# The last phase of a two-block layer: the sums of squares of keys and queries as two products of high and low parts, in the five passes 0 to 4, with the low parts made by GpSimd

## The chip, the cores and the metric

The kernel runs on one core of one Trainium2 chip. The metric is the device time of one execution, in microseconds (us). Lower is better. The program names five engines: TensorE (PE in the profile, PEld for its weight loads), VectorE (DVE), ScalarE (ACT), GpSimd (POOL) and SyncE (SP), which issues loads and stores. Each engine works through its own list of instructions strictly in order; semaphores are the only ties between lists. An instruction that waits therefore holds up everything behind it on its engine.

## The reference, cut to what matters

Two transformer blocks follow each other. The change lies in the second one, where queries and keys of every head are normalised over their 64 features before attention:

```
NORM_EPS = 1e-6
def rms_norm(t, g):
    tf = t.astype(jnp.float32)
    y = tf * lax.rsqrt(jnp.mean(tf * tf, axis=-1, keepdims=True) + NORM_EPS)
    return (y * g.astype(jnp.float32)).astype(t.dtype)
...
u = h @ w_in[i]
dq, dk, dv, bq, bk, bv, z = jnp.split(u, IN_SPLIT_IDX, axis=-1)
dq = rms_norm(dq.reshape(B, S, DIFF_HEADS, 2, HEAD_DIM), diff_q_norm_g[i])
dk = rms_norm(dk.reshape(B, S, DIFF_HEADS, 2, HEAD_DIM), diff_k_norm_g[i])
...
bq = rms_norm(bq.reshape(B, S, DIL_HEADS, HEAD_DIM), dil_q_norm_g[i])
bk = rms_norm(bk.reshape(B, S, DIL_HEADS, HEAD_DIM), dil_k_norm_g[i])
```

The sequence has 1024 positions, four differential heads (two queries and two keys of 64 features each) and eight dilated heads.

## The kernel before

**The phase.** The function `mixers_phase` runs eight passes p = 0 to 7, each over two times 64 features: passes 0 to 3 are the differential heads (DIFF = 4), passes 4 to 7 pairs of dilated heads. A pass has 16 units x = 0 to 15. A unit of pass p does the attention of pass p and, woven in, the projections of the next pass q = p + 1. The opening, p = -1, is 16 units that hold only the projections and key work of q = 0. The order of every engine's list is written out by hand: each engine has a loop over p and x, and small tables say what a unit holds.

**The projections.** For every q there are eight groups of 8 steps: GK0, GK1 (keys, two halves of 512 positions), GQ0, GQ1 (queries), GV0, GV1 (values), GZ0, GZ1 (gates). A step is `gemm_k`, three matmuls of 128x512 in type fp32r (lines 79 to 81: high by high, high by low, low by high). `share(q, x)` says which steps stand in a unit. For q of 1 and more GK0 ends in unit 1, GK1 with the first step of unit 3, GQ0 in unit 4, GQ1 in unit 6. In the opening the order is GK0, GQ0, GV0, GZ0, GK1, GQ1, GZ1, GV1; the first group has already been made by the phase before.

**The weights.** They come through two buffers. `W.split` on POOL turns one loaded tile of 128x1024 into a high part (line 135) and a low part (line 137); PE waits for it at a tile's first step, and the split waits until the tile that used the buffer before is done. In the opening, `opening = {1: 0, 2: 1, 3: 2, 4: 3, 5: 4, 7: 5, 9: 6}` sets in which unit POOL splits which; split 0 delivers the tile of the third group, GV0. In later passes a split stands in units 0, 4, 8 and 12.

**Keys and queries.** When a group of them is complete, ACT empties its PSUM bank (`empty`): the square into the tile `sq` (line 2472), a plain copy into `un` (line 2474, which frees the bank and counts `gfree`). PE sums the squares over 64 features by one matmul with the 0/1 matrix K.pairs (item "S", line 2262, plain fp32). ACT scales the sum (`halve`, line 2523) and forms the inverse root by Ln, Exp and a square (`inverse_root`, lines 2530 to 2541). DVE takes one correction step and scales `un` (`scale`, lines 2718 to 2722). POOL splits `un` in a high part (line 2195) and a low part (line 2201), in `split_rows`, and PE multiplies keys and queries (`keys`, line 2312; `scores`, lines 2347 and 2350). `sums_of` places the four S items of q in units 3, 4, 5 and 7 (in the opening 4, 5, 6 and 8), at the unit's head. `normed_at` places `scale` and `split_rows` one unit later each. `is_late` lists the items that stand behind the unit's second projection step instead.

**What else counts.** A unit's attention on DVE is `add` (line 2704), the maxima of `keys` for the next pass (line 2741) and `weigh` (line 2778); on PE it ends with `values` (line 2366), which needs the `weigh` of the unit before. `un`, `sq` have two buffers each, used in turn by the running number c of the group among keys and queries (`number_of`).

Of the kernel before, what the change touches and what calls it, by code (L numbers as in the profile page):

```python
# [5 lines left out]
F32 = mybir.dt.float32  # L6
F32R = mybir.dt.float32r
BF16 = mybir.dt.bfloat16
ALU = mybir.AluOpType
ACT = mybir.ActivationFunctionType  # L10
P = 128
D = 1024
T = 1024
META = 16
L = META + T
KT = D // P
# [1886 lines left out]

def mixers_phase(nc, K, u_hi, u_lo, strips, pt, S, V_p, acc0, o1, x1, row_of):

# [16 lines left out]
    order = lambda q: [GK0, GQ0, GV0, GZ0, GK1, GQ1, GZ1, GV1] if q == 0 else list(range(8))  # L1922
    place = lambda q, g: order(q).index(g)
    number_of = lambda q, g: 4 * q + [n for n in order(q) if n <= GQ1].index(g)
    tile_of = lambda q, g: place(q, g) if q == 0 else 4 * q + 4 + g // 2
# [47 lines left out]
    roots = {it: n for n, it in enumerate(it for it in number if it[0] in "SN")}  # L1973
    is_late = lambda p, x, it: it[0] == "E" and x == 6 or it[0] in ("D", "P", "EB", "EP") or it[0] == "T" and (p < 0 or x == 13)

# [27 lines left out]
    with ExitStack() as ctx:  # L2003
# [22 lines left out]
        stored = [s(f"stored{i}") for i in range(4)]  # L2026
        tok_ok = s("tokens")
        rootx, invx, scalex, addx_ok, sqx_ok, sumx = (s(n) for n in ["rootx", "invx", "scalex", "addx", "sqx", "sumx"])
# [152 lines left out]
        def _(pool):  # L2181
            def split_rows(q, g):
# [18 lines left out]
                nc.gpsimd.tensor_tensor(lo, new, hi.bitcast(F32), ALU.subtract).then_inc(lo_ok, 1)  # L2201

            def key_tokens(q, i):

                pool.wait_ge(lo_ok, 4 * q + 4)
                pool.wait_ge(mx_full, base(q) + 6)
                source = (k_hi, k_lo)[i][:, q % 2].bitcast(F32)
                nc.gpsimd.tensor_copy(turned(tok[:, i]), classes(source)).then_inc(tok_ok, 1)

            opening = {1: 0, 2: 1, 3: 2, 4: 3, 5: 4, 7: 5, 9: 6}  # L2210
            for p in range(-1, PASSES):
                q = p + 1
                for x in range(U):
                    if q < PASSES and x in normed_at(q):
                        split_rows(q, normed_at(q)[x])
                    if q < PASSES and not diff(q) and x in (13, 14):
                        key_tokens(q, x - 13)
                    if p < 0:
                        if x in opening:
                            W.split(pool, 0, 0, opening[x])  # L2220
                    elif x == 0:
                        W.split(pool, 0, 0, 4 * p + 7)
                    elif x in (4, 8, 12) and q < PASSES:
                        W.split(pool, 0, 0, 4 * q + 3 + x // 4)
# [9 lines left out]
        def _(pe):  # L2234
# [15 lines left out]
            def extra(it):  # L2250
# [9 lines left out]
                if kind == "S":  # L2260
                    pe.wait_ge(sq_ok, number_of(q, g) + 1)
                    last = nc.tensor.matmul(bank, K.pairs[:, :], sq[:, number_of(q, g) % 2], start=True, stop=True)
                if kind == "N":
# [147 lines left out]
            for p in range(-1, PASSES):  # L2411
                q = p + 1
# [49 lines left out]
        def _(act):  # L2462
            def empty(q, g):
# [5 lines left out]
                if g <= GQ1:  # L2469
                    c = number_of(q, g)  # L2470
                    least(act, un_ok, c - 1)
                    nc.scalar.activation(sq[:, c % 2], gbank(n), ACT.Square).then_inc(sq_ok, 1)
                    least(act, lo_ok, c - 1)
# [207 lines left out]
        def _(dve):  # L2681
# [178 lines left out]
            nc.vector.memset(mn[:, :], 0.0).then_inc(cleared, 1)  # L2860
            dve.wait_ge(cleared, 1)
            for j in range(2):
                last = nc.vector.memset(ek[64 * j:64 * j + 2, :].bitcast(F32), 1.0)
# [283 lines left out]
def program(nc, d, s):  # L3147
    K = Kernel(d, s)
    with ExitStack() as top:
# [36 lines left out]
        with ExitStack() as two:  # L3186
# [7 lines left out]
            with ExitStack() as c2:  # L3194
# [9 lines left out]
                W.base = W.base + 2 * KT  # L3204
                mixers_phase(nc, K, h_hi, h_lo, strips, pt, S, V_p, acc0, o1, x1, mix_row)
                clear_semaphores(nc)
# [104 lines left out]
```

## Time and profile before

| | before |
|---|---|
| median of 3 runs | 2913.04 us (2912.51 to 2915.86) |
| the profiled execution: time, span | 2912.82 us, 2911.0 us |
| mean granted clock of TensorE | 0.98 of 2.4 GHz |
| PE busy over the span | 2761.9 us (95%) |
| DVE, ACT, POOL busy | 1708.0 us (59%), 1045.7 us (36%), 935.9 us (32%) |
| the phase `mixers_phase` | about 1890 to 2720 us of the span |

A timeline row gives the start in us from the span's start, the duration in us, the engine, the line, the operation, the tiles (out<-in) with shape and count, and in brackets how long the engine stood idle before it and for whom. Matmuls are pipelined: the record of one overlaps the next, so what a matmul costs is the distance from start to start, not its duration. A plain fp32 matmul leaves two records. Busy shares are means over a stretch; what a change is worth is read from the waits.

### The profile page before, as it was taken

Reading aid. Unit: us, or ns where it says so; the run is one execution under the profiler, and the core shown is the slowest. Engines: PE = TensorE matmul, PEld = TensorE weight load, DVE = VectorE, ACT = ScalarE, POOL = GpSimd, SP = SyncE. Lnnn points to the kernel's source line nnn. Section 1 sums busy time; section 2 is a strip of 40 time slices with the busy share of each in tenths; the row PEclk is TensorE's granted clock in tenths of the full one; section 3 lists DMA queues with packets and bytes.
Section 4 is the critical chain, followed back from the end, with each engine's and each line's share of the span. In section 5 each row is a group of like instructions: output and inputs, shape, how many; then the busy total and the mean of one; then the engine's idle time right before and its main releaser. Section 6 shows DMA issues by size and latency. Waiting matters only on the chain. (4 is left out here: it accounts for less than half of the span.)

```text
span 2911.0 us, 39453 instructions
## 1 busy us (share of the span) xinstructions
PE 2761.9 (95%) x15534; PEld 2115.5 (73%) x15534; DVE 1708.0 (59%) x2674; ACT 1045.7 (36%) x1735; POOL 935.9 (32%) x549
## 2 busy tenths in 40 slices
PE   6999999999999899999999999979999999998899
PEld 5879797977777677777766887755666666665677
DVE  5787878786022344444454115666776667775586
ACT  4342524343010233333333002346666644344232
POOL 1233323332664122211212334542122234341465
PEclk8999999999999899999999999989999999999999
DMA  4131413244432111111113225421110111103544
GB/s 166 60 84 66 94 66 83 71 80 155 165 118 91 37 52 52 50 47 48 34 44 135 82 80 183 137 86 36 40 43 27 43 43 44 43 30 113 173 150 112
DMA packets 113751, 237.32 MB, mean 82 GB/s; under 512 B 9120, under 2 KB 52896, under 8 KB 113568
## 3 DMA queue, kind: packets, MB, share of 16 engines
q1 hardware_dynamic: 63312, 172.93, 17.9%
q10 hardware_dynamic: 50256, 61.87, 7.3%
q8 instruction: 124, 2.03, 0.3%
q14 instruction: 59, 0.48, 0.1%
HBM read 190.66 MB, written 44.11 MB: 81 GB/s over the span
## 5 line engine op out<-in xcount | busy, mean ns | idle before, releaser
L79 PE MATMUL psum<-u_h,w_hi 128*128 128x512 f32 (+2 forms) x2624 | 1012.7, 386 | 25.0 <-PEq L46 7.3
L80 PE MATMUL psum<-u_h,w_hi 128*128 128x512 f32 (+2 forms) x2624 | 968.4, 369 | 0.0
L81 PE MATMUL psum<-u_h,w_lo 128*128 128x512 f32 (+2 forms) x2624 | 966.3, 368 | 0.0
L135 POOL TENSOR_SCALAR w_hi<-w_raw 128x1024 fp32r<-128x1024 f32 x212 | 241.6, 1140 | 1468.6 <-ACTq L1324 519.1
L79 PEld LDWEIGHTS psum<-u_h,w_hi 128*128 128x128 f32 x2624 | 497.8, 190 | 156.1 <-issue 69.3
L137 POOL TENSOR_TENSOR w_lo<-w_raw,w_hi 128x1024 fp32r<-128x1024 f32 x212 | 546.1, 2576 | 17.7
L81 PEld LDWEIGHTS psum<-u_h,w_lo 128*128 128x128 f32 x2624 | 497.8, 190 | 71.8
L80 PEld LDWEIGHTS psum<-u_h,w_hi 128*128 128x128 f32 x2624 | 498.5, 190 | 69.3 <-issue 9.0
L2545 ACT ACTIVATE a_exp<-a_exp 128x1024 f32<-128x1024 f32 x96 | 101.6, 1058 | 161.9 <-DVE a_exp L2708 88.3
L1349 ACT ACTIVATE f_exp<-psum 128x1024 f32<-128x1024 f32 (+4 forms) x112 | 82.2, 734 | 192.9 <-PE psum L1207 94.0
L1445 DVE CUSTOM_DVE_ANT_0 f_junk<-psum,f_decay,f_max 128x512 f32<-128x512 f32 (+2 forms) x96 | 60.3, 666 | 134.4 <-PE psum L1230 121.1
L2704 DVE TENSOR_TENSOR a_exp<-psum,a_strips 128x1024 f32<-128x1024 f32 x64 | 78.2, 1222 | 74.2 <-PE psum L2350 73.5
L603 ACT ACTIVATE decay<-decay,ssd_small 128x128 f32<-128x128 f32 x256 | 78.4, 389 | 102.2 <-DVE decay L803 97.8
L79 PE MATMUL psum<-yo_hi,w_hi 128*128 128x512 f32 x256 | 100.8, 394 | 6.0 <-DVE yo_lo L1003 3.4
L80 PE MATMUL psum<-yo_lo,w_hi 128*128 128x512 f32 x256 | 100.4, 392 | 0.0
L81 PE MATMUL psum<-yo_hi,w_lo 128*128 128x512 f32 x256 | 100.2, 391 | 0.0
L1253 PE MATMUL psum<-f_exp,f_v 128*64 128x512 f32 (+4 forms) x448 | 89.0, 474 | 3.0 <-ACT f_exp L1349 3.0
L2195 POOL CAST a_khi<-a_un 128x512 fp32r<-128x512 f32 x16 | 15.6, 974 | 229.7 <-DVE a_un L2722 229.7
L2551 ACT ACTIVATE a_biased<-a_biased,a_negmax 128x1024 f32<-128x1024 f32 x60 | 68.5, 1144 | 45.0 <-DVE a_negmax L2748 45.0
L1003 DVE TENSOR_TENSOR yo_lo<-yo_raw,yo_hi 128x512 fp32r<-128x512 f32 x32 | 31.2, 1045 | 90.5 <-ACT yo_hi L951 90.5
L1460 DVE TENSOR_TENSOR f_sum<-f_sum,f_exp 128x800 f32<-128x800 f32 (+2 forms) x96 | 77.6, 809 | 7.1 <-ACT f_exp L1349 6.0
L1445 DVE CUSTOM_DVE_ANT_0 f_junk<-psum,f_decay 128x512 f32<-128x512 f32 (+4 forms) x128 | 48.8, 433 | 55.8 <-PE psum L1230 37.8
(433 smaller groups left out, 4419.3 us busy)
## 6 DMA issues: line engine op xcount, KB each, us to landing
w_raw<-in_w_all SPq DMA_DIRECT2D x212, 512.0 KB, 3.5
sums_rows<-s_acs ACTq DMA_DIRECT2D x32, 512.0 KB, 8.8
f_decay<-s_nc SPq DMA_DIRECT2D x16, 520.0 KB, 5.4
s_y<-conv_out ACTq DMA_DIRECT2D x16, 512.0 KB, 2.9
yo_raw<-s_y ACTq DMA_DIRECT2D x8, 1024.0 KB, 10.3
a_strips<-in_strips SPq DMA_DIRECT2D x8, 960.0 KB, 5.4
x_tok<-in_x SPq DMA_DIRECT2D x8, 512.0 KB, 8.2
s_xT<-xT SPq DMA_DIRECT2D x8, 512.0 KB, 6.0
```

The costliest lines, as they stand in the source:

```text
L79: nc.tensor.matmul(out, w_hi[:, k], a_hi, start=(k == 0 and first), stop=False)
L80: nc.tensor.matmul(out, w_hi[:, k], a_lo, start=False, stop=False)
L81: return nc.tensor.matmul(out, w_lo[:, k], a_hi, start=False, stop=(k == kk - 1 and final))
L135: self.nc.gpsimd.tensor_scalar(self.hi[:, r], self.raw[:, r], 1.0, 1.0, ALU.mult, ALU.mult).then_inc(self.hi_done, 1)
L137: self.nc.gpsimd.tensor_tensor(self.lo[:, r], self.raw[:, r], self.hi[:, r].bitcast(F32), ALU.subtract).then_inc(self.ready, 1)
L603: last = nc.scalar.activation(seg[:, d % 3, r], seg[:, d % 3, r], ACT.Exp, scale=-1.0, bias=sm[:, g, 0, d, r:r + 1])
L1253: last = nc.tensor.matmul(ps[64 * j:64 * j + 64, OB + q0:OB + 512], V[0:n, kb, j], pt[0:n, x % 2, j, q0:512], start=(kb == 0), stop=(kb == ...
L1349: nc.scalar.activation(pt[0:n, x % 2, :, q0:512], src[:, :, q0:512], ACT.Exp, scale=0.125).then_inc(exp_ok, 1)
L1445: last = nc.vector.tensor_tensor_reduce(out=junk[:, j, o:o + e - a], in0=ps[:, MX + 512 * j + o:MX + 512 * j + o + e - a], in1=ncb[:, j, a ...
L1460: nc.vector.tensor_tensor(to, to, src, ALU.add).then_inc(acc_ok, 1)
L2545: nc.scalar.activation(pt[:, X % 3], pt[:, X % 3], ACT.Exp, scale=0.125).then_inc(exp_ok, 1)
L2704: tt(pt[:, X % 3], bank, strips[:, p % 2:p % 2 + 1, o:o + 512].to_broadcast([P, 2, 512]), ALU.add).then_inc(add_ok, 1)
```

## The change

For every q up to DIFF (0 to 4, so for twenty of the thirty-two groups; `halved(q)`), the sum of squares is taken in two matmuls of type fp32r instead of one in fp32. ACT writes the square into the tile `tok`, which is fp32r and holds a rounded, high part. POOL forms the square again in full from the copy `un` (into `sq`) and subtracts the high part, which gives the low part (`squares_low`). PE multiplies both with `exact`, an fp32r copy of K.pairs that DVE makes once, in a free piece of the tile u_h. These S items become late: they stand behind the second projection step of their unit. PE waits for `low_ok`, POOL waits for `gfree`.

```
-    is_late = lambda p, x, it: it[0] == "E" and x == 6 or it[0] in ("D", "P", "EB", "EP") or ...
+    is_late = lambda p, x, it: it[0] == "S" and halved(it[1]) or it[0] == "E" and x == 6 or it[0] in ("D", "P", "EB", "EP") or ...
...
+            def squares_low(q, g):
+                c = number_of(q, g)
+                pool.wait_ge(sq_ok, c + 1)
+                pool.wait_ge(gfree, 8 * q + place(q, g) + 1)
+                nc.gpsimd.tensor_tensor(sq[:, c % 2], un[:, c % 2], un[:, c % 2], ALU.mult).then_inc(low_ok, 1)
+                pool.wait_ge(low_ok, 2 * c + 1)
+                nc.gpsimd.tensor_tensor(tok[:, 1, 512 * (c % 2):512 * (c % 2) + 512], sq[:, c % 2],
+                                        tok[:, 0, 512 * (c % 2):512 * (c % 2) + 512].bitcast(F32), ALU.subtract).then_inc(low_ok, 1)
...
                     if q < PASSES and x in normed_at(q):
                         split_rows(q, normed_at(q)[x])
+                    for g, k in share(q, x) if q < PASSES and halved(q) else []:
+                        if k == KT - 1 and g <= GQ1 and (q, g) != (0, GK1):
+                            squares_low(q, g)
+                    if (q, x) == (0, 5):
+                        squares_low(0, GK1)
...
                 if kind == "S":
-                    pe.wait_ge(sq_ok, number_of(q, g) + 1)
-                    last = nc.tensor.matmul(bank, K.pairs[:, :], sq[:, number_of(q, g) % 2], start=True, stop=True)
+                    c = number_of(q, g)
+                    if halved(q):
+                        pe.wait_ge(const_ok, 1)
+                        pe.wait_ge(low_ok, 2 * c + 2)
+                        for i in range(2):
+                            last = nc.tensor.matmul(bank, exact, tok[:, i, 512 * (c % 2):512 * (c % 2) + 512], start=(i == 0), stop=(i == 1))
+                    else:
+                        pe.wait_ge(sq_ok, c + 1)
+                        last = nc.tensor.matmul(bank, K.pairs[:, :], sq[:, c % 2], start=True, stop=True)
...
-                    nc.scalar.activation(sq[:, c % 2], gbank(n), ACT.Square).then_inc(sq_ok, 1)
+                    squares = tok[:, 0, 512 * (c % 2):512 * (c % 2) + 512] if halved(q) else sq[:, c % 2]
+                    nc.scalar.activation(squares, gbank(n), ACT.Square).then_inc(sq_ok, 1)
...
+            nc.vector.tensor_copy(exact, K.pairs[:, :])
```

The first place is POOL's list at the phase's start. Before, it begins with the weight splits:

```order
L2180 UNCONDITIONAL_BRANCH
L135 TENSOR_SCALAR w_hi<-w_raw 128x1024
L137 TENSOR_TENSOR w_lo<-w_raw,w_hi 128x1024
L135 TENSOR_SCALAR w_hi<-w_raw 128x1024
L137 TENSOR_TENSOR w_lo<-w_raw,w_hi 128x1024
```

In the changed kernel the two pairs of `squares_low` for GK0 and GQ0 (lines 2209 and 2211) stand there first:

```order
L2181 UNCONDITIONAL_BRANCH
L2209 TENSOR_TENSOR a_sq<-a_un 128x512
L2211 TENSOR_TENSOR a_tokens<-a_sq,a_tokens 128x512
L2209 TENSOR_TENSOR a_sq<-a_un 128x512
L2211 TENSOR_TENSOR a_tokens<-a_sq,a_tokens 128x512
L135 TENSOR_SCALAR w_hi<-w_raw 128x1024
L137 TENSOR_TENSOR w_lo<-w_raw,w_hi 128x1024
```

So split 0, the weights of GV0, has moved behind the squares of GQ0.

The second place is POOL's list in pass 0, from the split of the keys GK0 in unit 4 to the split of the queries GQ1 in unit 8. Before:

```order
L2195 CAST a_khi<-a_un 128x512
L2201 TENSOR_TENSOR a_klo<-a_un,a_khi 128x512
L135 TENSOR_SCALAR w_hi<-w_raw 128x1024
L137 TENSOR_TENSOR w_lo<-w_raw,w_hi 128x1024
L2195 CAST a_khi<-a_un 128x512
L2201 TENSOR_TENSOR a_klo<-a_un,a_khi 128x512
L2195 CAST a_qhi<-a_un 128x512
L2201 TENSOR_TENSOR a_qlo<-a_un,a_qhi 128x512
L2195 CAST a_qhi<-a_un 128x512
L2201 TENSOR_TENSOR a_qlo<-a_un,a_qhi 128x512
```

And now (lines 2196 and 2202 are the old 2195 and 2201):

```order
L2196 CAST a_khi<-a_un 128x512
L2202 TENSOR_TENSOR a_klo<-a_un,a_khi 128x512
L2209 TENSOR_TENSOR a_sq<-a_un 128x512
L2211 TENSOR_TENSOR a_tokens<-a_sq,a_tokens 128x512
L135 TENSOR_SCALAR w_hi<-w_raw 128x1024
L137 TENSOR_TENSOR w_lo<-w_raw,w_hi 128x1024
L2196 CAST a_khi<-a_un 128x512
L2202 TENSOR_TENSOR a_klo<-a_un,a_khi 128x512
L2196 CAST a_qhi<-a_un 128x512
L2202 TENSOR_TENSOR a_qlo<-a_un,a_qhi 128x512
L2209 TENSOR_TENSOR a_sq<-a_un 128x512
L2211 TENSOR_TENSOR a_tokens<-a_sq,a_tokens 128x512
```

The pair for GQ0 stands between the split of GK0 and the weights, and the pair for GQ1 behind the split of GQ0.

The third place is PE's list in the same pass, unit 3. Before, the S matmul stands ahead of scores and key products:

```order
L2366 MATMUL psum<-a_exp,a_v 128x512
L2262 MATMUL psum<-a_sq,pairs 128x512
L2347 MATMUL psum<-a_qhi,a_khi 128x512 x2
L2347 MATMUL psum<-a_qlo,a_khi 128x512 x2
L2347 MATMUL psum<-a_qhi,a_klo 128x512 x2
L2350 MATMUL psum<-a_queryrows,a_keyrows 128x512 x2
```

Now two matmuls stand behind the second projection step:

```order
L2335 MATMUL psum<-a_khi,a_qlo 128x512 x2
L79 MATMUL psum<-u_h,w_hi 128x512
L80 MATMUL psum<-u_h,w_hi 128x512
L81 MATMUL psum<-u_h,w_lo 128x512
L79 MATMUL psum<-u_h,w_hi 128x512
L80 MATMUL psum<-u_h,w_hi 128x512
L81 MATMUL psum<-u_h,w_lo 128x512
L2282 MATMUL psum<-a_tokens,u_h 128x512 x2
```

All S items of passes 0 to 4 move in this way, four in each; in unit 8 of the opening the item also falls behind the first key products.

## Rows read from the trace of the kernel before

**Rows 1.** Busy time in two stretches: opening of the last phase, and one pass.

```profile
core 0: us, PE busy (x) PEld busy (x) DVE busy (x) ACT busy (x) POOL busy (x), PEclk, DMA share, GB/s
1890.00:1990.00 100.00, 77.47 (x300) 50.21 (x299) 67.81 (x114) 46.79 (x77) 36.13 (x24) 0.90 0.25 88
1990.00:2090.00 100.00, 99.14 (x481) 64.94 (x480) 68.72 (x133) 63.08 (x97) 22.84 (x16) 1.00 0.10 33
```

**Rows 2.** Timeline of PE in unit 4 of pass 0, and one pass later.

```profile
2012.32 1.02 PE L2262 MATMUL psum<-a_sq,pairs 128*128 128x512 f32 x2
2013.27 0.50 PE L2347 MATMUL psum<-a_qhi,a_khi 64*128 64x512 f32 x2
...
2015.10 0.50 PE L79 MATMUL psum<-u_h,w_hi 128*128 128x512 f32 x1
2015.43 0.39 PE L80 MATMUL psum<-u_h,w_hi 128*128 128x512 f32 x1
2015.66 0.39 PE L81 MATMUL psum<-u_h,w_lo 128*128 128x512 f32 x1
...
2112.07 1.02 PE L2262 MATMUL psum<-a_sq,pairs 128*128 128x512 f32 x2
```

**Rows 3.** Timeline at the phase's start: weight split, second drain, next projection.

```profile
1892.45 2.38 POOL L137 TENSOR_TENSOR w_lo<-w_raw,w_hi 128x1024 fp32r<-128x1024 f32 x1
...
1906.44 0.59 ACT L2474 ACTIVATE a_un<-psum 128x512 f32<-128x512 f32 x1
...
1906.97 0.80 PE L79 MATMUL psum<-u_h,w_hi 128*128 128x512 f32 x1
```

**Rows 4.** Instructions of lines 2195 and 2201 on POOL: min/median/max in ns.

```profile
L2195 POOL CAST a_khi<-a_un x16: 611/1086/1497, 1941.3 to 2589.6; 128x512 fp32r<-128x512 f32 x16
...
L2201 POOL TENSOR_TENSOR a_klo<-a_un,a_khi x16: 1262/1406/2067, 1942.0 to 2590.8; 128x512 fp32r<-128x512 f32 x16
```

**Rows 5.** Timeline of pass 0 around the drains, splits and sums of squares.

```profile
2011.89 0.59 ACT L2474 ACTIVATE a_un<-psum 128x512 f32<-128x512 f32 x1
...
2018.56 1.27 POOL L2201 TENSOR_TENSOR a_klo<-a_un,a_khi 128x512 fp32r<-128x512 f32 x1
...
2019.31 1.10 PE L2262 MATMUL psum<-a_sq,pairs 128*128 128x512 f32 x2 [0.33 <-ACT a_sq L2472]
2019.87 0.60 ACT L2474 ACTIVATE a_un<-psum 128x512 f32<-128x512 f32 x1 [0.70 <-POOL a_klo L2201]
...
2032.49 1.29 POOL L2201 TENSOR_TENSOR a_qlo<-a_un,a_qhi 128x512 fp32r<-128x512 f32 x1
```

**Rows 6.** Timeline of the opening's second half.

```profile
1943.26 0.60 ACT L2474 ACTIVATE a_un<-psum 128x512 f32<-128x512 f32 x1 [1.42 <-POOL a_klo L2201]
...
1951.86 1.02 PE L2262 MATMUL psum<-a_sq,pairs 128*128 128x512 f32 x2
...
1954.51 0.50 PE L2312 MATMUL psum<-a_khi,a_qhi 64*128 64x512 f32 x2 [1.63 <-POOL a_klo L2201]
...
1959.86 0.75 DVE L2741 CUSTOM_DVE_ANT_0 a_biased<-psum,a_strips,a_max 128x512 f32<-128x512 f32 x1
...
1977.93 0.63 PE L2279 MATMUL psum<-ident,a_maxrows 128*128 128x128 f32 x4 [3.51 <-DVE a_maxrows L2797]
```

**Rows 7.** Timeline of PE behind an idle stretch in the opening.

```profile
1944.49 1.25 PE L2262 MATMUL psum<-a_sq,pairs 128*128 128x512 f32 x2 [2.64 <-ACT a_vT L2523]
...
1946.38 0.63 PE L81 MATMUL psum<-u_h,w_lo 128*128 128x512 f32 x1
...
1948.87 0.39 PE L81 MATMUL psum<-u_h,w_lo 128*128 128x512 f32 x1
```

**Rows 8.** Timeline of DVE and POOL where both work on SBUF tiles.

```profile
2019.77 1.61 DVE L2778 SCALAR_TENSOR_TENSOR a_exp<-a_exp,neglam 128x512 f32<-128x512 f32 x1
...
2020.93 2.72 POOL L137 TENSOR_TENSOR w_lo<-w_raw,w_hi 128x1024 fp32r<-128x1024 f32 x1
...
2031.20 0.75 DVE L2778 SCALAR_TENSOR_TENSOR a_exp<-a_exp,neglam 128x512 f32<-128x512 f32 x1
```

More of the change, by code:

```diff
@@ L1901, in _, with mixers_phase @@
             split(KT - 1)
-def mixers_phase(nc, K, u_hi, u_lo, strips, pt, S, V_p, acc0, o1, x1, row_of):
+def mixers_phase(nc, K, u_hi, u_lo, exact, strips, pt, S, V_p, acc0, o1, x1, row_of):
     PASSES, DIFF, U, SPAN = 8, 4, 16, 2 * T - P
@@ L1923, in mixers_phase @@
     place = lambda q, g: order(q).index(g)
+    halved = lambda q: q <= DIFF
     number_of = lambda q, g: 4 * q + [n for n in order(q) if n <= GQ1].index(g)
@@ L1973, in mixers_phase @@
     roots = {it: n for n, it in enumerate(it for it in number if it[0] in "SN")}
-    is_late = lambda p, x, it: it[0] == "E" and x == 6 or it[0] in ("D", "P", "EB", "EP") or it[0] == "T" and (p < 0 or x == 13)
+    is_late = lambda p, x, it: it[0] == "S" and halved(it[1]) or it[0] == "E" and x == 6 or it[0] in ("D", "P", "EB", "EP") or it[0] == "T" and (p < 0 or x == 13)
     def scored(p, x):
@@ L2026, in mixers_phase @@
         stored = [s(f"stored{i}") for i in range(4)]
-        tok_ok = s("tokens")
+        tok_ok, low_ok = s("tokens"), s("squares_low")
         rootx, invx, scalex, addx_ok, sqx_ok, sumx = (s(n) for n in ["rootx", "invx", "scalex", "addx", "sqx", "sumx"])
@@ L3204, in program @@
                 W.base = W.base + 2 * KT
-                mixers_phase(nc, K, h_hi, h_lo, strips, pt, S, V_p, acc0, o1, x1, mix_row)
+                mixers_phase(nc, K, h_hi, h_lo, uh[:, 2 * KT * T:2 * KT * T + P], strips, pt, S, V_p, acc0, o1, x1, mix_row)
                 clear_semaphores(nc)
```

## The prediction

> **What bounds the kernel now.** I read first the busy shares by stretch, then the timeline of every engine in two places: the opening of the phase, and one whole pass, with the waits beside each row. In the 100 us from 1990 on, which is one pass, PE is busy for 99.14 us at a granted clock of 1.00, DVE for 68.72, ACT for 63.08 and POOL for only 22.84 [rows 1]. So in the passes PE is the bound: each microsecond taken from its list comes back, and each one in which it must stand still is lost. The opening is another matter. There PE is busy for 77.47 of 100 us, and the end is set by a chain that goes PE, ACT, DVE, POOL and back [rows 1]. The passes repeat: the S of unit 4 stands at 2012.32 and, one pass later, at 2112.07 [rows 2], so what I work out for pass 0 holds for the four passes p = 0 to 3 which make q = 1 to 4; the opening makes q = 0.
>
> **What is taken from PE.** The S matmul starts at 2012.32 and the next one at 2013.27, so it takes 0.95 us of PE's list [rows 2]. An fp32r matmul of the same 128x512 takes 0.23, the distance from 2015.43 to 2015.66 [rows 2]; two are 0.46. The saving is 0.49 for each item, 1.96 for each of the four passes. One old wait of 0.33 for ACT's square goes too [rows 5]. That makes -2.3 for a pass, if the low parts are there in time.
>
> **What POOL's two instructions cost.** The trace has no product of a tile with itself on POOL. The nearest row is the subtraction of 128x512 on the same engine, 1262 ns at best and 1406 in the median; the one-input cast of the same shape has 611 at best, and that is my lower bound for either instruction, the 2067 of the slowest subtraction the upper one [rows 4]. A product of two inputs is nearest to the subtraction, and I take 1.3 for each, 2.6 for the pair: between 1.3 and 4.1.
>
> **The opening, first wait.** POOL's list is in order, and split 0, the weights of GV0, now stands behind the pair for GQ0. That pair waits for ACT's copy of GQ0, which ends at 1906.44 + 0.59 = 1907.03; before, POOL had the weights done at 1892.45 + 2.38 = 1894.83, and PE began GV0 at 1906.97 [rows 3]. Now: 1907.1 + 2.6 for the pair + 1.1 and 2.4 for the split (its second half took 2.38 [rows 3]; its first half lies between the end of a split at 2018.56 + 1.27 [rows 5] and the second half's start at 2020.93 [rows 8]) + 0.2 between them gives 1913.4. PE waits 6.4 us there. The group holds the sums that the second half of the normalised input depends on, which DVE and ACT then work through while PE waits for them, so nothing takes this back: +6.4. If each instruction of the pair were as cheap as the cast it would be 5.0, with slow ones 7.9.
>
> **The opening, second wait.** From here on I use the times of before, without the 6.4. The pair for GK1 can start when its copy is done, at 1943.26 + 0.60 = 1943.86 [rows 6], and ends at 1946.5. Behind it come in POOL's order the weights (3.5, to 1950.0), the split of GQ0 (0.61 + 1.27, to 1952.0), ACT's copy of GQ1, which waits for that (to 1952.7), its pair (to 1955.3), and the split of GK1 (to 1957.3). Before, the first key products followed that split at 1954.51 [rows 6]. They come 2.8 later. The S of GQ1 stood at 1951.86, before them [rows 6]; now it stands behind them and two steps, at about 1957.3 + 1.0 + 2.4 = 1960.7, with the steps at the slower clock as they are now. From its S to DVE's second maximum, which stands behind the scaling of GQ1, took 1951.86 to 1959.86 [rows 6]; with 0.4 less for the matmul and 1.3 less for waits on the way the maximum comes at about 1967, 7 late. DVE and PE work together until the queries' rows are turned at 1977.93, where PE waits 3.51 us for DVE [rows 6]. On the way DVE has, by its timeline, some 3 us of waits that it can make up (an estimate). That leaves +3.8; I add 0.8 for the shared tiles (below) and take +4.6, between 1 (the casts' price) and 6. The opening costs 6.4 + 4.6 = 11.0. S savings count nothing here, since PE stands idle around them.
>
> **A pass.** Take pass 0.
> - GK1: ACT's copy ended at 2011.89 + 0.59 = 2012.48 [rows 5], now 0.2 later, as ACT serves the later S of GK0 first. The pair ends at 2012.8 + 2.6 = 2015.4. PE begins unit 4 at 2011.84 (2012.32 less 0.49 saved in unit 3), needs 1.83 for scores and keys (2013.27 to 2015.10 [rows 2]) and 1.38 for two steps, six times 0.23, and is at the S at 2015.05: a wait of 0.4.
> - GQ0: its copy waits for the split of GK0, which ends at 2018.56 + 1.27, and is done at 2019.87 + 0.60 = 2020.47 [rows 5]. The pair ends at 2023.1. PE begins unit 5 at 2018.4 (2018.98 as it was, 0.33 before the S at 2019.31 [rows 5], less 0.98 saved, plus the 0.4 of above, rounded) and is at its S 1.13 + 1.38 later, about 2020.8: a wait of 2.3.
> - GQ1: POOL first splits GQ0, which ended at 2032.49 + 1.29 = 2033.8 [rows 5] and is now 0.6 later, as unit 6 is. The pair ends at 2034.4 + 2.7 = 2037.1. PE is at its S at 2031.4 + 1.13 + 1.38 = 2033.9: a wait of 3.1.
> - GK0 has more than a unit of cover and costs nothing.
>
> Together 5.8 of waits against 2.3 of savings: +3.5. With the casts' price for the pair each of the two large waits is 1.3 shorter and the small one gone, and the pass is at +0.5; at 4.1 for the pair it is at +8.
>
> **Two things that waits bring with them.** First the clock. After PE had been idle for 2.64 us, up to 1944.49, its matmuls took 0.63 each, until one at 1948.87 has 0.39 again [rows 7]: the granted clock had gone from 2.4 to 1.2 GHz for some 3.5 us. In these a matmul starts every 0.43 instead of every 0.23, which loses 1.6. The wait of GQ1 is as long as that one; the wait of GQ0 is shorter, and I count it as harmless. I take 1.3 a pass, between 0 and 3.2. Second, tiles that POOL and DVE both work on. DVE's `weigh` took 1.61 us at 2019.77, against 0.75 at 2031.20; it ended only after POOL's first half of a weight split was over, and the second half, begun at 2020.93, took 2.72 instead of the 2.38 above [rows 8, 3]. They hold each other up. In the changed kernel this weight split begins at 2023.1 and ends at about 2026.7, just where DVE has the small rows of unit 5 and scales GK1. The scaling comes up to 2 us later, then unit 6's add, the scaling of GQ0, its split, the pair and the S. Part of it has slack, and I take +1.0, between 0 and 2.
> The Trainium skill, page "SBUF — State Buffer", section "Who interferes with whom", says that a DVE instruction with two SBUF inputs and a GpSimd instruction that reads SBUF fully block each other, whichever issued first. The trace agrees, with the 1.61 us. By that rule alone nothing is shared and the whole 2 us would come through, 4 us more in all than I count.
>
> A pass: 3.5 + 1.3 + 1.0 = 5.8, four of them 23.2. Pass 3, which makes q = 4, has one more cast on POOL between the splits of GQ0 (0.6), so its pair is later by that: +0.6. The copy `exact` on DVE is 128x128 in a stretch where DVE next waits for a load: nothing; without that cover it would be about 0.2.
>
> **The sum.** 11.0 + 23.2 + 0.6 = +34.8 against the profiled execution, 2912.82, gives 2947.6. Its time lies within 0.3 us of the median of the three runs. I say 2947 us, 1.2% slower.
>
> **The rivals.**
> - *The waits of the passes are small; only the opening is slower.* If POOL's pair takes 1.3 to 1.7, a pass is at about +0.5 to +1 and the opening at 5.0 + 1.5: 2912.8 + 6.5 + 3 = 2922. For it speaks the cast's 0.61 [rows 4]; against it that both instructions have two inputs and none such of this shape was under 1.26. Chance 0.11.
> - *The loss is larger, because POOL and DVE block each other everywhere.* The pair itself collides with `scale`, `add`'s successors and `weigh`; by the page's rule every such meeting costs the length of the other's instruction. With 3.4 for the pair, 2 for the shifted weight split and a slow clock behind both waits, a pass costs 3.5 + 2.4 + 2 + 1.6 = 9.5: 2912.8 + 13 + 38 = 2964. DVE has 31 us of free time in a pass [rows 1], which speaks against all of it coming through. Chance 0.15.
> - *Faster.* PE's list gets 20 times 0.49 = 9.8 us shorter, with old waits some 11, and everything else is covered: 2902. It decides at the price of POOL's pair: at 0.5 us a pass would gain 1.1 (the wait of GQ1 would still be 1.0, as PE is at its S 0.5 before POOL starts the pair) and the opening lose 4.3, which is even; only below that is the kernel faster. The cast alone has 0.61 [rows 4]. Chance 0.03.
> - *No change within the measure*: gains of the passes even with the opening's loss, which needs a pass at -2.3 and an opening of 9. Chance 0.03.
>
> **How the numbers follow.** The forecast case, waits of both kinds with 2930 to 2960, has 0.68. A measurement of this kernel can tell about 0.2%, 6 us, from no change. Slower by more: 0.68 + 0.11 + 0.15 = 0.94; within: 0.03; faster: 0.03. The range takes the lower bound of a pass with a quick pair (a pass at 3, the opening at 8: 2933) and goes down to 2929, and up to 2962, which holds about half of the case of blocking; outside remain the first rival and the rest of the second, with the two small ones some 0.2 in all.
>
> **What the profile after would show.** Step by step: PE idle for about 6 us before its first step of GV0, released by POOL's line 137; the pair at 1.3 us each; in each of the passes 0 to 3 waits of PE for POOL's line 2211 in units 4, 5 and 7, near 0.4, 2.3 and 3.1, so some 23 us over the four; matmuls of 0.63 behind the third; DVE's scaling lengthened where the weight split meets it. Wrong would be: a pair much shorter than 2.6; a PE that reaches its S later than I reckon, because DVE holds it up in the scores, which would turn one wait into another; or an opening whose chain has slack that I have not seen.

## The result, and the profile after

The changed kernel takes 2958.43 us (median of 4 runs, 2957.19 to 2959.70) against 2912.78 for the kernel before on the same chip: 1.0155 times as long, 95% interval 1.0139 to 1.0171. The prediction was 2947 us, in a range of 2929 to 2962. The profiled execution took 2957.19 us, with a span of 2955.4 and a mean granted clock of 0.973.

The busy shares of the changed kernel, in the opening and in one pass, answer to [rows 1]:

```profile
core 0: us, PE busy (x) PEld busy (x) DVE busy (x) ACT busy (x) POOL busy (x), PEclk, DMA share, GB/s
1890.00:2001.00 111.00, 77.57 (x271) 51.16 (x272) 60.48 (x103) 40.62 (x68) 43.54 (x31) 0.80 0.22 74
2001.00:2107.00 106.00, 98.08 (x473) 64.49 (x470) 73.13 (x136) 63.86 (x98) 30.62 (x23) 0.97 0.09 28
```

PE does no more work than before; it stands idle for some 8 us of a pass, where it had stood idle for less than one. POOL is busy for only 30.62 of the 106 us, so its load is not what holds PE up, but when its pieces come. The list of PE's waits over the whole phase names the places (line waited at, releaser, us in total, times, longest):

```profile
PE psum L2282 <- POOL a_tokens L2211: 26.4, 9, 5.5
PE psum L2335 <- POOL a_klo L2202: 7.1, 1, 7.1
...
PE psum L79 <- POOL w_lo L137: 6.0, 1, 6.0
...
PE psum L2370 <- ACT a_queryrows L2543: 4.5, 4, 1.1
```

Line 2282 is the new S item. The last row stands at a place that the forecast does not name: the scores (line 2370) wait for ACT four times, once a pass.

**The opening.** The timeline at the phase's start, POOL and PE, answers to [rows 3]:

```profile
1906.58 1.48 POOL L2209 TENSOR_TENSOR a_sq<-a_un 128x512 f32<-128x512 f32 x1 [11.42 <-ACT a_un L2498]
1908.14 1.26 POOL L2211 TENSOR_TENSOR a_tokens<-a_sq,a_tokens 128x512 fp32r<-128x512 f32 x1
...
1910.49 2.34 POOL L137 TENSOR_TENSOR w_lo<-w_raw,w_hi 128x1024 fp32r<-128x1024 f32 x1
...
1912.97 0.76 PE L79 MATMUL psum<-u_h,w_hi 128*128 128x512 f32 x1 [6.04 <-POOL w_lo L137]
1913.54 0.63 PE L80 MATMUL psum<-u_h,w_hi 128*128 128x512 f32 x1
```

PE waits 6.04 us for the weights, where the prediction had 6.4, and the matmuls behind it start 0.43 us apart until 1917.81: the granted clock has gone to the 1.2 GHz level. And in its second half, to be laid beside [rows 6]:

```profile
1954.57 0.70 PE L2282 MATMUL psum<-a_tokens,u_h 128*128 128x512 f32 x2 [3.77 <-POOL a_tokens L2211]
1955.53 2.69 POOL L137 TENSOR_TENSOR w_lo<-w_raw,w_hi 128x1024 fp32r<-128x1024 f32 x1
1955.90 2.87 DVE L2743 SCALAR_TENSOR_TENSOR a_un<-a_un,a_par,a_sq 128x512 f32<-128x512 f32 x1
1967.41 0.79 PE L2335 MATMUL psum<-a_khi,a_qhi 64*128 64x512 f32 x2 [7.10 <-POOL a_klo L2202]
...
1994.14 1.09 PE L2302 MATMUL psum<-ident,a_maxrows 128*128 128x128 f32 x4 [3.51 <-DVE a_maxrows L2821]
```

DVE's scaling of GQ0 takes 2.87 us instead of 0.74 (in the kernel before it starts at 1947.16), because it meets the second half of the weight split, which runs from 1955.53 to 1958.22 and which the pair has pushed into it. The rows are turned at 1994.14, which was 1977.93 before.

**A pass.** Units 4 to 7 of pass 0, all four engines, beside [rows 2, 5, 8]:

```profile
2033.03 0.70 PE L2282 MATMUL psum<-a_tokens,u_h 128*128 128x512 f32 x2
2040.25 0.70 PE L2282 MATMUL psum<-a_tokens,u_h 128*128 128x512 f32 x2 [1.58 <-POOL a_tokens L2211]
2041.20 2.38 POOL L137 TENSOR_TENSOR w_lo<-w_raw,w_hi 128x1024 fp32r<-128x1024 f32 x1
2041.37 2.24 DVE L2814 TENSOR_TENSOR a_lse<-a_logsum,a_negmax 128x8 f32<-128x8 f32 x1
2043.64 0.17 DVE L2816 CAST a_lse_hi<-a_lse 128x8 fp32r<-128x8 f32 x1
...
2049.72 0.50 PE L2370 MATMUL psum<-a_qhi,a_khi 64*128 64x512 f32 x2 [1.12 <-ACT a_queryrows L2543]
...
2052.00 1.27 POOL L2202 TENSOR_TENSOR a_qlo<-a_un,a_qhi 128x512 fp32r<-128x512 f32 x1
2053.23 1.04 POOL L2209 TENSOR_TENSOR a_sq<-a_un 128x512 f32<-128x512 f32 x1
2054.35 1.26 POOL L2211 TENSOR_TENSOR a_tokens<-a_sq,a_tokens 128x512 fp32r<-128x512 f32 x1
...
2055.76 1.19 PE L2282 MATMUL psum<-a_tokens,u_h 128*128 128x512 f32 x2 [3.25 <-POOL a_tokens L2211]
2056.75 0.63 PE L79 MATMUL psum<-u_h,w_hi 128*128 128x512 f32 x1
```

The first row is GK1, with no wait that the view marks (0.26 us in the next pass); GQ0 waits 1.58, GQ1 3.25, with the slow clock behind it. Between them, DVE's sum over eight elements takes 2.24 us: it begins at 2041.37 and ends at 2043.61, POOL's second half of the split at 2043.58. The next one of that size takes 0.17, with POOL idle by then. All that DVE has behind it, the scaling of GK1, the add of unit 6 and with it the exponentials on ACT, is late by these 2 us; ACT copies the query rows behind the exponentials, and for this copy the scores wait.

**A ledger.** To see where each kernel's time differs I take the start of each value product (before: line 2366; one a unit) and subtract its start in the kernel before, counted from the same product. The opening is counted from PE's first matmul of the phase (1890.80 before) to the second value product (1997.54 before); a pass from there on over 16 products, the last over 13. The table gives the opening's length and what each pass is longer, in us, worked out from the PE timelines of the profiled executions. "Keys", "place" and so on are the experiments below.

| kernel | opening | pass 0 | pass 1 | pass 2 | pass 3 |
|---|---|---|---|---|---|
| before | 106.74 | 0 | 0 | 0 | 0 |
| changed | 124.34 | +7.05 | +5.96 | +5.94 | +9.57 |
| opening only | 121.00 | 0.00 | 0.00 | +0.03 | +0.19 |
| passes only | 105.39 | +5.96 | +5.97 | +5.95 | +9.52 |
| keys only | 104.85 | +0.25 | +0.19 | +0.19 | 0.00 |
| place only | 106.88 | +0.79 | +0.70 | +0.69 | +1.48 |
| GK0 alone, at the head | 104.94 | -0.37 | -0.36 | -0.41 | -1.54 |
| split 0 first | 116.48 | +7.15 | +5.95 | +5.94 | +9.63 |
| GQ1 first | 124.56 | +2.52 | +2.53 | +2.53 | +2.95 |
| squares by ACT | 118.91 | +3.69 | +2.09 | +3.62 | +4.33 |
| three of four | 107.29 | +0.34 | +0.34 | +0.34 | +0.27 |
| three, weights in unit 3 | 107.42 | -1.24 | -1.25 | -1.27 | -2.34 |

The unchanged openings lie between 104.85 and 107.42, so a difference under 3 us there says nothing. Counted from the start of the span instead, the second value product stands at 1997.48 to 2000.06 with an unchanged opening, at 2014.99 to 2017.09 with the changed one, and at 2012.97 with split 0 first: a late start of the phase and a short opening go together in part, so a change of the opening is known only to 2 or 3 us by either count. In pass 3 differences of 1.2 us come and go with a wait that has nothing to do with the change. In passes 0 to 2 the table repeats within 0.1 us or so wherever the clock does. For the changed kernel it adds up to 17.6 + 28.5 = 46.1 us; 1.4 of that comes back in passes 4 to 7 (as in experiments 3, 4 and 12, so it is not a gain of the change), and the spans differ by 44.4.

### The profile page after: what moved, and what is told of

Its sections match the earlier page's. It is cut to its first block and busy times, and to the rows that moved or that the text cites. A ratio compares the mean times of both kernels' runs of the same rounds, so it can differ in the third digit from the quotient of the medians.

```text
span 2955.4 us, 39513 instructions
## 1 busy us (share of the span) xinstructions
PE 2769.1 (94%) x15534; PEld 2122.7 (72%) x15534; DVE 1717.1 (58%) x2675; ACT 1047.6 (35%) x1735; POOL 982.7 (33%) x589
## 5 line engine op out<-in xcount | busy, mean ns | idle before, releaser
L388 POOL TENSOR_TENSOR x_dt_decay<-x_dt,ssd_small 128x512 f32<-128x512 f32 (+1 forms) x32 | 36.8, 1152 | 129.3 <-DVE x_dt L789 128.8
```

## The experiments

The lines below are of each kernel's own file, so the same instruction has a number a few apart.

**1. The opening alone.**

```
-    halved = lambda q: q <= DIFF
+    halved = lambda q, g: q == 0
```

> The two products and the low parts only for q = 0, the opening; passes 0 to 3 as before. My theory: the losses of the opening and of the passes are separate and add up. In the trace of the changed kernel the queries' rows of the opening are turned at 1994.14 instead of 1977.93, 16.2 us later, so this kernel should take 2912.8 + 16.2 = 2929.0. Rival 1: the opening costs the 11.0 of my prediction and the rest arises only with the passes: 2924. Rival 2: the passes, with their waits gone, take part of the delay back: 2920 to 2925.

Measured: 2929.75 us, ratio 1.0060 (1.0046 to 1.0073), 18 us above the kernel before on that chip (2911.66). Its passes are at zero in the ledger. So the opening costs 18 us and not the 11.0 of the prediction. The ledger shows 14 to 16 of them in this execution, which entered the phase late (PE's first matmul at 1894.60; over all kernels here it lies between 1890.65 and 1896.49, with no relation to the change that I can see).

**2. The passes alone.**

```
+    halved = lambda q, g: 0 < q <= DIFF
```

> The two products only for q = 1 to 4, made in passes 0 to 3; the opening as before. My theory: what is left of the 45.6 us, 29.4, so 2942. Rival: the passes cost the 23.8 of my prediction: 2936.6. In the trace the waits of the S items for POOL's line 2211 should be as they are now: about 1.6 in unit 5, 3.3 in unit 7, and 1.1 of the scores for ACT's copy of the rows.

Measured: 2938.92 us, ratio 1.0095 (1.0080 to 1.0111): +27.3. The two parts add up, 18.1 + 27.3 = 45.4. The prediction had 23.8 for the passes. Passes 0 to 2 take 5.96 each, 0.2 more than the forecast of 5.8; the rest is pass 3 with 9.5.

**3. Only the keys of q = 1 to 4,** GK0 and GK1.

```
+    halved = lambda q, g: 0 < q <= DIFF and g <= GK1
```

> Only the keys GK0 and GK1 of q = 1 to 4 get two products; the queries and the opening stay as before. My theory: the keys' low parts are covered, so eight items give 0.49 each, less 0.26 of waiting for GK1 in four passes: 3.9 - 1.0 = 2.9 us faster, 2910. Rival: POOL's pair holds up DVE's scaling of GK0 (its first instruction took 1.60 us instead of 0.69 in the changed kernel), which comes back as waits: 2913 or slower.

Measured: 2913.57 us, ratio 1.0006 (0.9997 to 1.0015): nothing is gained, though both pairs are ready in time. Within pass 0 the ledger stands at -0.40 behind GK0, at -0.46 behind GK1, and at +0.29 behind GQ0, whose plain S now waits 1.10 us for ACT's square instead of 0.33.

**4. The same two items only moved,** still plain fp32, nothing on POOL.

```
+    is_late = lambda p, x, it: it[0] == "S" and 0 < it[1] <= DIFF and it[2] <= GK1 or it[0] == "E" and x == 6 or ...
```

> The kernel before, with the S items of GK0 and GK1 of q = 1 to 4 only moved behind the second projection step: still one plain fp32 matmul of a_sq, nothing on POOL. Theory: the late place itself costs, because ACT comes to the inverse root of GK1 later and drains GQ0 behind it (in the run with both keys changed PE's wait at the S of GQ0 was 1.10 us against 0.33). A pass is then 0.6 to 1.2 us longer, the total 2914.5 to 2916.5 us. Rival: the place costs nothing, and the gain of the run with both keys was eaten by POOL's pair: 2911.7 us.

Measured: 2914.03 us, ratio 1.0007 (0.9998 to 1.0016). The times alone can't tell the two theories apart, the ledger does: 0.7 to 0.8 us more a pass, all of it at the S of GQ0, whose row is

```profile
2022.04 1.10 PE L2262 MATMUL psum<-a_sq,pairs 128*128 128x512 f32 x2 [1.09 <-ACT a_sq L2472]
```

ACT's list is in order too: it forms the inverse root of GK1 ahead of the drain of GQ0, so an S that comes 3.4 us later in unit 4 (2017.67, less the 1.91 by which this execution is later, against 2012.32) makes the next square 0.8 us late (2021.31 less 1.91, against 2018.59). With the cheap matmuls the same pass is at +0.25. The late place had a price of its own, 0.8 us a pass, for which the prediction had nothing.

**5. GK0 alone, at its old place** at the head of unit 3, where POOL has over a unit for the pair.

```
+    halved = lambda q, g: 0 < q <= DIFF and g == GK0
     is_late = lambda p, x, it: it[0] == "E" and x == 6 or ...
```

> The kernel before, with only GK0 of q = 1 to 4 made of high and low parts, and its S item left at the unit's head: POOL has more than a unit for its pair. Theory: the saving of 0.49 us an item comes through in full where nothing is moved and nothing waited for: 4 x 0.49 = 2.0 us less, 2909.7 us, and unit 3 is 0.49 us shorter in the trace. Rival: ACT's chain in unit 4 sets the time, and the wait at the S of GQ0 grows by what was gained: 2911.7 us.

Measured: 2911.93 us, ratio 1.0000 (0.9992 to 1.0009). In the ledger each of passes 0 to 2 is 0.36 to 0.41 shorter and keeps it. So the saving exists and comes through, but 1.5 us in all is below what the measurement can tell.

**6. In the opening, the weights first:** split 0 ahead of the pair for GQ0, the rest as changed.

```
+                    if p < 0 and x in (0, 1):
+                        if x == 0:
+                            squares_low(q, GK0)
+                        else:
+                            W.split(pool, 0, 0, opening[x])
+                            squares_low(q, GQ0)
```

> The changed kernel with one thing swapped: in the opening POOL makes weight split 0 before the pair of GQ0. My theory: the wait of 6.03 us for the weights of GV0 goes, and with it the slow clock behind it (eight matmuls at 0.43 instead of 0.23, 1.6 us): 2958.4 - 7.6 = 2950.8. Rival 1: only the wait goes, since the clock is low there anyway: 2952.4. Rival 2: the chain of the second half is bound elsewhere and takes it back: above 2955.

Measured: 2953.14 us, ratio 1.0141 (1.0128 to 1.0155), against 1.0155 (1.0139 to 1.0171) for the whole change: 4 to 5 us less, though the two intervals overlap. PE's wait for the weights is gone, and the opening is 7.9 us shorter (124.34 to 116.48), more than the wait's 6.04, since the slow matmuls behind it go too. The profiled execution entered the phase 5.8 us later than that of the changed kernel (1896.49 against 1890.65), which is why its total shows only 1.7 of it. That the medians show 4 to 5 and not 7.9 is not explained. What is left, 116.48 against 104.85 to 107.42, is 9 to 12 us by the ledger (by the times, 18 less 4 to 5, it would be 13 to 14), and belongs to the second half: PE still waits 3.63 at the S of GK1 and 6.99 at the first key products, and DVE's scaling of GQ0 still takes 2.88.

**7. In the passes, GQ1's pair ahead of the split of GQ0** (q = 1 to 4; the opening as changed).

```
+                    if 0 < q < PASSES and halved(q) and x == 6:
+                        squares_low(q, GQ1)
                     if q < PASSES and x in normed_at(q):
                         split_rows(q, normed_at(q)[x])
```

> The whole change, with POOL's pair for GQ1 moved ahead of the split of GQ0 in unit 6 of passes 0 to 3 (the opening stays). Theory: the pair is ready in time, what delays it is the 2.4 us split ahead of it. PE's wait at the S of GQ1 falls from 3.3 to about 0.7 us, the slow clock behind it goes, and the keys' products of unit 6 wait some 0.6 us for the split of GQ0, which now comes last. A pass is 2.5 to 3 us shorter, pass 3 (with the additional cast between them) about 5: 2943 us. Rival: the wait only moves, to the key products behind the split of GQ0, and the clock falls there: 2955 or more.

Measured: 2939.89 us, ratio 1.0097 (1.0083 to 1.0111): 28.5 us above the kernel before on that chip instead of 45.7, so 17 us come from the order of two pieces on POOL (18 in the ledger). The waits of PE and POOL's instructions in unit 7 are now:

```profile
2054.52 1.26 POOL L2211 TENSOR_TENSOR a_tokens<-a_sq,a_tokens 128x512 fp32r<-128x512 f32 x1
...
2056.41 1.29 POOL L2202 TENSOR_TENSOR a_qlo<-a_un,a_qhi 128x512 fp32r<-128x512 f32 x1
```
```profile
2055.93 0.70 PE L2284 MATMUL psum<-a_tokens,u_h 128*128 128x512 f32 x2 [1.35 <-POOL a_tokens L2211]
2057.95 0.50 PE L2337 MATMUL psum<-a_khi,a_qhi 64*128 64x512 f32 x2
```

The wait falls from 3.25 to 1.35, not to 0.7: the product takes 1.56 us here, beside DVE. The key products find the split of GQ0 done. A pass falls from 5.96 to 2.53, 1.9 from the wait and 1.5 from the clock, which now stays up in passes 0 to 2; pass 3 falls from 9.5 to 2.95, although there the clock falls behind GQ0's wait of 2.44. The wait of the scores (1.13) is unchanged.

**8. The full square by ACT,** so that POOL only subtracts (the rest as changed).

```
-                nc.gpsimd.tensor_tensor(sq[:, c % 2], un[:, c % 2], un[:, c % 2], ALU.mult).then_inc(low_ok, 1)
...
+                        nc.scalar.activation(squares, gbank(n), ACT.Square)
+                        nc.scalar.activation(sq[:, c % 2], gbank(n), ACT.Square).then_inc(sq_ok, 1)
```

> The whole change, but ACT writes the square twice (rounded into the tokens tile, in full into a_sq), so POOL's product of 1.04 us goes and its subtraction needs no copy of the rows. Theory: POOL's time in front of the S items is what costs. The wait for GQ0 (1.6) goes, the weight split of unit 4 comes 1.9 us earlier and no longer covers DVE's eight-element rows, so the 1.1 us wait of the scores goes too, GQ1's wait falls from 3.3 to 2.2; the opening is 3 us shorter. 4 x 3.8 + 3 = 18 us: 2940 us. Rival: ACT's 0.6 us more for each group delays the drains as much as POOL gains: 2952 or more.

Measured: 2939.62 us, ratio 1.0101 (1.0086 to 1.0116). The sum came out as expected, which is in part luck, since its parts did so only in part: GQ0's wait fell to 0.35 and GQ1's to 2.14, but the scores wait longer, 1.53 instead of 1.12. The weight split came earlier and still covered DVE's small sums, only another one of them (1.67 us, until the split's end).

**9. The weight split out of that place, first try:** experiment 7 with the split of unit 4 behind the split of GQ0 in unit 6.

```
+                    elif x == 6 and q <= DIFF:
+                        W.split(pool, 0, 0, 4 * q + 4)
```

> The change with GQ1's pair first (as in the run before), and in passes 0 to 3 the weight split of unit 4 moved on POOL behind the split of GQ0 in unit 6; PE needs these weights in unit 7. Theory: in the changed kernel the split's second half covers DVE's eight-element rows in unit 5 (one took 2.23 us instead of 0.17), which makes add, exps and ACT's copy of the query rows late; that is the 1.13 us wait of the scores. It goes, and PE reaches the S of GQ1 earlier, where the pair is earlier too by as much: 1.1 us a pass, 4.5 in all: 2935.5 us. Rival: the rows are late for another reason, the wait stays, and PE waits for the weights in unit 7 besides: 2940 us or more.

Measured: 2969.39 us, ratio 1.0198 (1.0184 to 1.0212), a loss. One half of the theory holds: DVE's six instructions over eight elements take 0.17 each, and the scores don't wait for ACT. But PE needs the weights at the first projection step of unit 7, and POOL's pair and split of unit 6, behind which they now stand, run when PE is there already (from 2050.01 to 2054.28). That I had not laid side by side:

```profile
2055.38 2.34 POOL L137 TENSOR_TENSOR w_lo<-w_raw,w_hi 128x1024 fp32r<-128x1024 f32 x1
```
```profile
2057.86 0.77 PE L79 MATMUL psum<-u_h,w_hi 128*128 128x512 f32 x1 [7.23 <-POOL w_lo L137]
```

**10 and 11. Three of the four groups,** q = 1 to 4: GK0 at the unit's head, GQ0 and GQ1 late, GK1 as before the change; ACT writes both squares, GQ1's subtraction first. Experiment 10 has the weights in unit 4 as before, 11 in unit 6.

```
+    halved = lambda q, g: 0 < q <= DIFF and g in (GK0, GQ0, GQ1)
+    is_late = lambda p, x, it: it[0] == "S" and halved(it[1], it[2]) and it[2] != GK0 or ...
```

> The opening and GK1 as before the change. For q = 1 to 4 GK0 (item at the unit's head), GQ0 and GQ1 (items late) in high and low parts; ACT writes both squares, POOL only subtracts, GQ1's subtraction ahead of the split of GQ0. Theory: with the single subtraction ready in time every saving comes through: 0.38 for GK0, 0.49 for GQ1, up to 0.8 for GQ0 (its old wait of 0.33 goes too), less what the weight split, 1.3 us later, costs DVE's rows, about 0.3: some 1.3 us a pass, 2911.4 - 5.3 = 2906 us. Rival: ACT's second square and the late place delay the next drain, and the wait comes back at the scores of unit 6: 2911 us or more.

> The last kernel with the weight split of unit 4 moved behind the split of GQ0 in unit 6 as well. Theory: POOL is then free in unit 5 and DVE's rows are not held up; up to 1.7 us a pass below the kernel before: 2904.6 us, 1 to 1.5 us below the run with the split in unit 4. Rival: the weights come late for unit 7 (PE waits for POOL's line 137 there), nothing is gained over the other: 2906 us or more.

Measured: 2914.42 us, ratio 1.0008 (0.9999 to 1.0017) with the weights in unit 4, and 2947.41 us, ratio 1.0120 (1.0106 to 1.0133), in unit 6, where PE waits 7.15 us for them as in experiment 9. With the weights in unit 4 no changed S waits more than 0.24 in pass 0, and behind GQ0 the ledger is at -1.39. Then the scores lose all of it:

```profile
2023.70 2.37 POOL L137 TENSOR_TENSOR w_lo<-w_raw,w_hi 128x1024 fp32r<-128x1024 f32 x1
```
```profile
2024.31 1.79 DVE L2813 TENSOR_TENSOR a_max<-a_max,a_sum 128x8 f32<-128x8 f32 x1 [0.47 <-ACT a_max L2587]
```
```profile
2032.60 0.50 PE L2370 MATMUL psum<-a_qhi,a_khi 64*128 64x512 f32 x2 [1.58 <-ACT a_queryrows L2547]
```

**12. The same with the weights one unit earlier,** in unit 3, where POOL has nothing and DVE stood idle.

```
+                    elif x == 3 and q <= DIFF:
+                        W.split(pool, 0, 0, 4 * q + 4)
```

> The kernel with three of four groups changed in q = 1 to 4 (ACT writes both squares, POOL subtracts, GQ1 first), now with the weight split of unit 4 one unit earlier, in unit 3, where POOL and DVE both have nothing to do (DVE stood idle for 4.07 us there). Theory: what ate the gain of the run with the split in unit 4 (2914.4 us) was DVE's eight-element rows held up until POOL's second half of the split was over; with the split gone from there the 1.58 us wait of the scores goes, and each pass is 1.3 to 1.7 us shorter than in the kernel before: 2905 to 2906 us, and PE does not wait for the weights, as it does when they are split in unit 6. Rival: the split is late for another reason (its buffer or its load), or DVE's scaling in unit 4 is held up in turn and the GQ0 bank drained later: 2911 us or more.

Measured: 2908.05 us (11 runs) against 2911.87 (15 runs) on the same chip, ratio 0.9987 (0.9978 to 0.9996): faster than the kernel before, by 3.8 us. The three places that were slow in the run before now read:

```profile
2013.36 2.38 POOL L137 TENSOR_TENSOR w_lo<-w_raw,w_hi 128x1024 fp32r<-128x1024 f32 x1
```
```profile
2024.41 0.17 DVE L2815 TENSOR_TENSOR a_max<-a_max,a_sum 128x8 f32<-128x8 f32 x1 [0.47 <-ACT a_max L2589]
```
```profile
2031.08 0.50 PE L2372 MATMUL psum<-a_qhi,a_khi 64*128 64x512 f32 x2 [0.19 <-ACT a_queryrows L2549]
```

Passes 0 to 2 are 1.24 to 1.27 us shorter than before, nearly all of the 1.39 that stood in the ledger behind GQ0. Of pass 3's 2.34 some 1.2 is the wait that comes and goes, so the ledger vouches for about 5 us over the four passes. The forecast of 2905 to 2906 was some 2 us too low. This is an arrangement of its own: how much of its gain a move of the weights alone would bring in the kernel before wasn't tried.

## Why the prediction was right, and where its terms were off

The mechanism was right: PE's list gets shorter, and it loses several times that in waits for POOL, at the places named. The forecast was 11 us too low because terms of the sum were too small: the opening cost 18 us and not 11.0, the passes 27.3 and not 23.8. That passes 0 to 2 came out at 5.96 against 5.8 is partly luck, since the saving and GQ0's wait were both put too high, and these two errors cancel.

- **The saving of an item** is 0.40 and not 0.49. The prediction read it from the distance between the start of the S and the next start, but that distance depends on which matmul follows. At its old place the S can be compared like with like, from the value product ahead of it to the scores behind it, in the kernel before and in experiment 5:

```profile
2004.29 1.02 PE L2366 MATMUL psum<-a_exp,a_v 128*128 128x512 f32 x2
2005.15 1.02 PE L2262 MATMUL psum<-a_sq,pairs 128*128 128x512 f32 x2
2006.10 0.50 PE L2347 MATMUL psum<-a_qhi,a_khi 64*128 64x512 f32 x2
```
```profile
2006.82 1.02 PE L2390 MATMUL psum<-a_exp,a_v 128*128 128x512 f32 x2
2007.27 1.03 PE L2283 MATMUL psum<-a_tokens,u_h 128*128 128x512 f32 x2
2008.24 0.50 PE L2371 MATMUL psum<-a_qhi,a_khi 64*128 64x512 f32 x2
```

From value product to scores it is 1.81 before and 1.42 with the two products, while from the S to the scores it is 0.95 and 0.97. The ledger has the same 0.37 to 0.41 behind GK0 wherever it is changed. In the late place a plain S also starts only 0.46 ahead of the next matmul (experiment 4), so the step from 2132.79 to 2133.25 of the changed kernel is no measure of the saving.

- **POOL's pair**, taken as 2.6, is 1.04 for the product and 1.26 for the subtraction in the median of 20, so 2.3. The bounds held; the choice was 0.3 too dear, which hid a little of the rest.
- **The opening's first wait**, 6.4 forecast, is 6.04. But PE's clock fell behind it, and ten matmuls started 0.43 instead of 0.23 apart, 2 us. I had counted the slow clock only in the passes. Experiment 6 gives the whole term back, as 7.9 in the ledger and 4 to 5 in the times.
- **The opening's second wait**, 4.6 forecast, is about 10 by the ledger (experiment 6: 116.48 against 104.85 to 107.42). The term that was mis-sized most is this chain through GQ0: I let the pair push the weight split, and did not ask what DVE does at its new time. It scales GQ0 there, and takes 2.87 instead of 0.74; behind this stand the split of GQ0, the drain and pair of GQ1 and the split of GK1. The key products wait 7.10 instead of 1.63, and the later S of GQ1 is behind them. Counted from PE's first matmul, experiment 6 has the first key products 5.2 us later than the kernel before (68.88 against 63.71), where the prediction had 2.8, and the S of GQ1 12.1 later (73.18 against 61.06), where it had 8.8. How the 10 divide between the lengthened scaling, the slow clock and DVE's slack was not separated.
- **GK1 in a pass**: 0.4 forecast, 0.26 measured (the ledger has 0.06 left of its 0.40), but its late place delays ACT's inverse root and the next drain. Experiment 4 prices that at 0.8 a pass with a plain S. In the changed kernel it is mostly hidden, because GQ0's S waits for POOL anyway.
- **GQ0**: 2.3 forecast, 1.58 to 1.66 measured (2.42 in pass 3), in part by the quicker pair.
- **GQ1**: 3.1 forecast, 3.25 to 3.29 measured. That it is the order behind the split of GQ0 is shown by experiment 7.
- **The clock**: 1.3 a pass forecast. In pass 1 the stretch from the scores of unit 6 to behind GQ1 costs 5.5 us; the two waits are 1.13 + 3.29 and the S saves 0.40, which leaves 1.5. In pass 0 the same sum leaves 2.6.
- **POOL and DVE at the same time**, in the prediction "tiles that both work on" (they are not the same tiles: POOL has w_raw and w_hi, DVE has a_logsum and a_negmax): +1.0 forecast, 1.12 to 1.15 measured, as a wait of the scores for ACT's copy of the query rows, at a place that I had not named. Experiments 9, 11 and 12 remove it, but for 0.2 to 0.4, by moving the weight split, and 10 has it at 1.58 without POOL's product, so it is shown. The Trainium skill, page "SBUF — State Buffer", section "Who interferes with whom", has the rule that a DVE instruction with two SBUF inputs and a GpSimd instruction that reads SBUF block each other; it makes no difference for size, and the trace agrees, as a sum of 128x8 elements was held for 2.07 us. The prediction would have let the whole 2 us come through by that rule. In the wait of the scores 1.1 of them appears; whether the rest is slack or stands in GQ1's wait, whose pair hangs on DVE's scaling too, was not separated. Between experiments 10 and 12 nearly all comes through: the sum was held for 1.62, and a pass is 1.58 shorter without it.
- **Pass 3**: +0.6 forecast, 3.6 measured above pass 2. The splits of the dilated heads' keys and queries are slower: a cast has 1.13 to 1.49 us there and a subtraction 1.51 to 2.06, which lie between the medians and the upper ends of [rows 4]; I had reckoned every split with 0.61 + 1.27. So GQ0 waits 2.42 and GQ1 5.51.

The first rival (small waits) fell with the pair's 2.3 us. The second, blocking everywhere, put the total at 2964 and is in part what happened: not a longer pair, but the shifted weight split meeting DVE at two places, in the opening and in unit 5 of each pass.

## What to carry to other kernels

Before work is put into an idle engine's list, look at the order and not at the share: here POOL was 23% busy, and the same twenty pairs cost 45.7 us in one order and 28.5 in another. Follow the piece that the new work pushes away as carefully as the new work itself: the largest error of this forecast lies in the opening, where a weight split that was pushed back by the pair landed on DVE's scaling. And where a saving is to be taken, begin with the items that have cover (GK0 had a unit of it, GK1 had none) and give the pushed-away work a place where both engines are idle.

## What the runs showed of the hardware

- A DVE sum of 128x8 elements with two SBUF inputs takes 0.17 us, and 2.24, 1.79 and 1.67 where it met the second half of POOL's weight split (changed kernel, experiments 10 and 8); each time it ended within 0.03 us of POOL's instruction. The kernel before has a milder case, 0.44 at 2023.24.
- POOL multiplies a 128x512 tile by itself in 1.04 us and subtracts two such tiles in 1.26 (medians of 20), though both are instructions of two operands.
- After idle stretches of 3.25 and 6.04 us PE's matmuls ran at the lower clock level for several us. After shorter ones it went both ways: after 1.58 they did not in pass 0 of the changed kernel, but did in pass 3 of experiment 10, where they start 0.43 apart from 2335.72 on; after 2.42 they did not in pass 3 of the changed kernel, but after 2.44 they did in pass 3 of experiment 7. In experiment 8 the same wait, 2.14 and 2.16 us, was followed by matmuls 0.43 apart in pass 0 and 0.23 apart in pass 1, and the pass was longer by 3.69 in one and 2.09 in the other. So the length of one wait does not tell what the clock does behind it.
